# First attention of a two-layer encoder: filling products in pieces of three, weight slots exchanged singly

## Chip, core and metric

The kernel runs on one core of one Trainium2 chip. The metric is the device time of one execution in microseconds. A core has five engines that run side by side and meet only at semaphores: TensorE (PE in the profile; its weight loads are PEld), VectorE (DVE), ScalarE (ACT), GpSimd (POOL) and SyncE (SP), which issues most DMAs.

## What is computed

Two layers over a sequence of 1024 tokens of width 1024. The change lies in layer 0, whose mixer is:

```python
def even_mixer(xn, w_in, w_out, w_s, b_s, ln_g, ln_b, rel_bias):
    proj = xn @ w_in
    a_u, a_v, b_q, b_k, b_v, i_q, i_k, i_w = jnp.split(proj, splits, axis=-1)
    a_out = gmlp_spatial_gate(gelu(a_u), gelu(a_v), w_s, b_s, ln_g, ln_b)   # 1024 wide
    b_out = dsa_attention(q, k, v, iq, ik, iw, rel_bias)                    # 16 heads of 64
    return jnp.concatenate([a_out, b_out], axis=-1) @ w_out                 # 2048 -> 1024
```

`dsa_attention` picks 256 keys for each query with an indexer and attends over them with a relative bias. All 16 heads share one key and one value head. The output projection has 2048 inputs: the first 1024 (a_out) are there before the attention begins, the last 1024 are its result.

## The kernel before

Every product is done in split precision: each operand is a rounded high part and a low rest, and a product is three matmuls (high x high, high x low, low x high), or two where one operand is stacked. ScalarE rounds, VectorE or POOL subtract.

**The first attention** goes in 32 steps (i,b): head group i of four heads (i = 0 to 3), query block b of 128 tokens (b = 0 to 7), with b + 1 key tiles of 128. On TensorE (`pe_attn0`, L2637) a step is: the logits of the next step's heads 0 and 1, then for each key tile `st` four transposes of the probabilities (one per head, L2675) into one of two PSUM banks, a further head of the next step's logits behind tiles 1 and 2 (in short steps the rest behind the denominators), and from tile 2 on the value product of tile `st - 2` (two matmuls); then the denominators (L2684) and the last two value products. A transposed tile is copied and rounded by ScalarE (L1670), its low part is made by VectorE (L2237), and only that frees the bank and lets the value product go. VectorE also adds the mask to the logits and takes the row minimum, in a far part (L2202) and a near part of up to 256 keys (L2217), and takes ScalarE's exponentials (L1647) on from there by a reciprocal. It divides the output (L2271). ScalarE makes the output's high half (`out_high`, L1650) at key tile 2 of the next step, and POOL (`pool_attn0`, L1195) does the rest of the split in three operations (L1211 to L1216); POOL also makes each step's mask with bias (L1115). SP (`sp_attn`, L748) stores each split output to `cat_scratch`.

**The fills.** While this runs, TensorE also does half of the output projection: the 1024 rows of `w_out` that meet a_out. A fill k (0 to 31) is one token tile by one half of the columns, over four of the eight weight tiles: 4 x 3 = 12 matmuls into PSUM bank 7 (`fill`, L2617). Fills 0 to 15 use weight tiles 0 to 3, fills 16 to 31 tiles 4 to 7. The stationary side is a unit tile (token tile u = k // 2, two buffers, loaded by `fill_units` L740 two units ahead, once fill 2u - 3 has been taken). VectorE takes a finished fill out of PSUM (`take_fill`, L2222), adding for k >= 16 the part sum of fill k - 16, which SP has stored and loaded again (`after_fill`, L759). The places are set by `fill_steps` (L104): block 0 none, blocks 1 to 4 one fill, blocks 5 to 7 two, until 16 are done in a pair of head groups. So (1,6), (1,7), (3,6), (3,7) have none. Within a step, `fill_plan` (L2651) gives six matmuls ahead of the first transposes, and the rest behind in lumps of three or six:

```python
if len(fills) == 2:
    return {0: (fills[0], 0, 2), 1: (fills[0], 2, 4), 5: (fills[1], 0, 2), "end": (fills[1], 2, 4)}
k = fills[0]
return {0: (k, 0, 2), min(2, keys - 1): (k, 2, 3), "end": (k, 3, 4)}
```

**The weight slots.** Four slots hold split weight tiles. Tile n is rounded by ScalarE (`split_hi`, L402) once `tile_done(n - 4)` (L360) says that its slot is free, and subtracted by POOL (`split_lo`, L412). For the fills that is the end of fill 15 or 31. The exchange for fills 16 to 31 stands at the end of (1,6) and in (1,7) on both engines; that for the next weights at the end of (3,6) and in (3,7). The rest of the projection (`pe_out`, L2803) begins after step (3,7), with the last heads' outputs loaded as stationary operand `hidden`.

## Time and profile before

| what | value |
|---|---|
| median of 3 runs | 2545.99 us (2543.73 to 2550.15) |
| profiled execution: span from first to last instruction | 2557.9 us |
| PE busy | 2427.4 us, 95% of the span, 11680 matmuls |
| DVE, ACT, POOL busy | 1694.0, 1183.7, 1472.5 us (66%, 46%, 58%) |
| DMA | 369.64 MB, 145 GB/s |
| first attention | 466 to 808 us of the span |

For the profiled execution only the span is shown, no time around it; it is 11.9 us above the median of the runs. Busy time of PE counts matmuls that are pipelined, with modelled ends, so a high share does not say that nothing is lost between them; start times do. "Idle before" names what ended the idle time.

### The profile page before, as it was taken

To read this page: it belongs to the slowest core of one execution; us is meant where nothing else is said; L and a number is where in the kernel's file an instruction comes from. 1 tells how busy PE (TensorE), PEld (TensorE's weight loads), DVE (VectorE), ACT (ScalarE), POOL (GpSimd) and SP (SyncE) were. 2 spreads that over 40 slices of the span, in tenths; PEclk is the share of its full clock that TensorE was granted. 3 is DMA by queue.
4 is the path that set the end of the run, shared out by engine and by line. 5 is a ranking of instruction groups with operands and counts; after the bars stand their busy time and mean duration, and the time that the engine had idled before them with its cause. 6 is when DMAs were issued, how large, how long until landed. Compare 5 with 4: busy or idle time off the path is not lost.

```text
span 2557.9 us, 34068 instructions
## 1 busy us (share of the span) xinstructions
PE 2427.4 (95%) x11680; PEld 1996.4 (78%) x11680; DVE 1694.0 (66%) x2859; ACT 1183.7 (46%) x2025; POOL 1472.5 (58%) x817
## 2 busy tenths in 40 slices
PE   7899999898998999999999999989989999999997
PEld 5689888777776778888778887867777888878886
DVE  5469998667775486655666676167758655576676
ACT  5442533556664274444333236265555444434331
POOL 2111578645553129887678642357725887578951
PEclk9999999899999999999999999989999999999999
DMA  5380643733544624455644444755553454754343
GB/s 150 63 129 26 134 101 125 238 103 100 157 131 163 214 86 140 140 168 151 238 165 162 141 134 128 169 148 136 133 186 99 146 167 138 240 199 146 115 140 132
DMA packets 324244, 369.64 MB, mean 145 GB/s; under 512 B 13874, under 2 KB 222290, under 8 KB 322052
## 3 DMA queue, kind: packets, MB, share of 16 engines
q1 hardware_dynamic: 315476, 351.96, 47.2%
q10 hardware_dynamic: 8352, 15.21, 2.0%
q8 instruction: 83, 1.36, 0.2%
q0 software_dynamic: 272, 0.62, 0.1%
q14 instruction: 61, 0.50, 0.1%
HBM read 237.18 MB, written 130.55 MB: 144 GB/s over the span
## 4 chain that ended last, share of the span: by engine, by line
PE 75%; DVE 6%; POOL 6%; DMA 4%; issue 4%; ACT 4%; SPq 1%; POOLq 0%; DVEq 0%; ACTq 0%
PE ps L462 72%; PE ps L2675 2%; POOL attn_out_split L1239 1%; POOL attn_out L1237 1%; DMA hidden<-cat_scratch 1%; DMA cat_scratch<-attn_out_split 1%; ACT relu_scores L1508 1%; DVE masks L2068 1%; POOL w_split L417 1%; PE ps L579 1%; DMA h_operand_raw<-h_operand_scratch 1%; POOL attn_out_split L1235 1%; DVE logits L2202 1%; ACT junk L1349 1%; POOL attn_out_low L1232 1%
## 5 line engine op out<-in xcount | busy, mean ns | idle before, releaser
L462 PE MATMUL ps<-xn_T,w_split 128*128 128x512 f32 (+1 forms) x2928 | 679.7, 391 | 2.2 <-ACT x_sums L1386 1.4
L462 PEld LDWEIGHTS ps<-xn_T,w_split 128*128 128x128 f32 (+1 forms) x2928 | 548.6, 188 | 121.2 <-DVE xn_T L2001 2.7
L417 POOL TENSOR_TENSOR w_split<-w_raw,w_split 128x1024 fp32r<-128x1024 f32 x78 | 199.5, 2568 | 484.4 <-ACT w_split L410 484.0
L462 PE MATMUL ps<-w_operand,h_operand 128*128 128x512 f32 x2016 | 461.6, 391 | 11.4 <-DVE acc L2471 7.5
L462 PEld LDWEIGHTS ps<-w_operand,h_operand 128*128 128x128 f32 x2016 | 379.8, 189 | 93.2 <-issue 10.7
L1263 POOL TENSOR_TENSOR w_split<-w_raw,w_split 128x512 fp32r<-128x512 f32 x168 | 242.2, 1454 | 105.5 <-ACT w_split L1766 104.0
L462 PE MATMUL ps<-x_sums_high,w_split 128*128 128x512 f32 x896 | 285.0, 389 | 0.0
L1295 POOL TENSOR_TENSOR w_operand<-w_block,w_operand 128x2048 fp32r<-128x2048 f32 x42 | 207.4, 4938 | 110.9 <-ACT w_operand L1786 110.9
L2473 DVE TENSOR_TENSOR acc<-acc,ps 128x512 f32<-128x512 f32 x288 | 185.4, 680 | 123.7 <-PE ps L462 123.5
L462 PE MATMUL ps<-w_split,hidden 128*128 128x512 f32 x960 | 228.8, 400 | 18.2 <-DMA hidden<-cat_scratch 7.1
L462 PEld LDWEIGHTS ps<-w_split,hidden 128*128 128x128 f32 x960 | 184.8, 194 | 59.5 <-issue 10.6
L1773 ACT ACTIVATE h_operand<-h_operand_raw 128x2048 fp32r<-128x2048 f32 (+1 forms) x56 | 95.3, 1703 | 266.5 <-DMA h_operand_raw<-h_operand_scratch 266.5
L2403 DVE TENSOR_TENSOR h_operand<-h_operand_raw,h_operand 128x2048 fp32r<-128x2048 f32 (+1 forms) x56 | 165.8, 2962 | 58.8 <-ACT h_operand L1773 58.8
L462 PEld LDWEIGHTS ps<-x_sums_high,w_split 128*128 128x128 f32 x896 | 168.2, 188 | 35.0
L1766 ACT ACTIVATE w_split<-w_raw 128x512 fp32r<-128x512 f32 x168 | 104.9, 629 | 167.7 <-PE ps L462 163.9
L462 PE MATMUL ps<-x_sums_low,w_split 128*128 128x512 f32 x448 | 174.3, 389 | 0.0
L2088 DVE TENSOR_SCALAR_CACHE_REDUCE sel_flag<-masks,sel_bound 128x1024 uint8<-128x1024 f32 (+2 forms) x192 | 168.9, 942 | 1.1
L462 PE MATMUL ps<-w_split,unit_tile 128*128 128x512 f32 x576 | 159.3, 408 | 0.5
L1670 ACT ACTIVATE probs_T<-ps 128x512 fp32r<-128x512 f32 x144 | 83.3, 593 | 121.4 <-PE ps L2675 116.5
L1349 ACT ACTIVATE junk<-acc 128x1024 f32<-128x1024 f32 x60 | 63.5, 1059 | 154.9 <-DVE acc L2370 138.3
L2237 DVE TENSOR_TENSOR probs_T<-ps,probs_T 128x512 fp32r<-128x512 f32 x144 | 98.0, 687 | 48.6 <-ACT probs_T L1670 47.7
L1301 POOL TENSOR_TENSOR w_block<-w_block,w_block 128x2048 f32<-128x2048 f32 x24 | 129.2, 5385 | 0.0
(279 smaller groups left out, 4252.0 us busy)
## 6 DMA issues: line engine op xcount, KB each, us to landing
h_operand_raw<-h_operand_scratch SPq DMA_DIRECT2D x42, 1024.0 KB, 5.4
w_raw<-in_w SPq DMA_DIRECT2D x72, 512.0 KB, 8.0
w_block<-in_w SPq DMA_DIRECT2D x48, 512.0 KB, 5.7
q_scratch<-q_split SPq DMA_DIRECT2D x128, 128.0 KB, 2.6
cat_scratch<-attn_out_split SPq DMA_DIRECT2D x128, 128.0 KB, 2.6
w_raw<-in_w_in SPq DMA_DIRECT2D x30, 512.0 KB, 5.4
q_tile<-q_scratch ACTq DMA_DIRECT2D x58, 256.0 KB, 2.7
h_operand_scratch<-h_even SPq DMA_DIRECT2D x14, 1024.0 KB, 4.4
```

Source lines behind the costliest of these rows:

```text
L417: nc.gpsimd.tensor_tensor(whl[:, n0 % 4, 1, :], wraw[:, n0 % 4, :], whl[:, n0 % 4, 0, :].bitcast(F32), ALU.subtract).then_inc(w_lo, 1)
L462: return nc.tensor.matmul(out_ap, stat, mov, start=start, stop=stop)
L1263: nc.gpsimd.tensor_tensor(w1_split(L, k, 1), w1_operand(L, k), w1_split(L, k, 0).bitcast(F32), ALU.subtract).then_inc(w1_lo, 1)
L1295: nc.gpsimd.tensor_tensor(w_split2(z, 1), w_operand2(z), w_split2(z, 0).bitcast(F32), ALU.subtract).then_inc(w2_lo, 1)
L1301: nc.gpsimd.tensor_tensor(dst, x, y, op).then_inc(w2_sum, 1)
L1349: nc.scalar.activation(junk[:], src, ACT.Square, scale=0.5 * D ** -0.5, accum_out=ss[:, t:t + 1]).then_inc(n_jk, 1)
L1766: nc.scalar.activation(w1_split(L, k, 0), w1_operand(L, k), ACT.Copy).then_inc(w1_hi, 1)
L1773: nc.scalar.activation(h_split(z, 0), h_split(z, 1, raw=True), ACT.Copy).then_inc(h2_hi, 1)
L2088: return tick(nc.vector.tensor_scalar(flag[:, n % 2, 0:(picks[k] + 1) * P], row(picks[k]), bound[:, k:k + 1].bitcast(F32), None, op, ALU.a ...
L2237: nc.vector.tensor_tensor(pT[:, x % 4, 1, :], ps[:, 4 + y % 2, :], pT[:, x % 4, 0, :].bitcast(F32), ALU.subtract).then_inc(c_free, 1)
L2403: nc.vector.tensor_tensor(h_split(z, 1), h_split(z, 1, raw=True), h_split(z, 0).bitcast(F32), ALU.subtract).then_inc(h2_lo, 1)
L2473: last = nc.vector.tensor_tensor(e, e, o, ALU.add)
```

## The change

The 32 fills become 128 pieces of three matmuls (one weight tile each). A plan made once gives every piece its place: four ("start") between the first step's second and third logits; in block 0 two ahead of the transposes ("pre"), one behind the tile, one at the end; in block 1 one "pre", one behind each tile, one at the end; in blocks 2 to 7 one behind each of the last n key tiles, where n comes from a list, (more than b + 1 go to "pre", which happens only in (3,2)). Step (3,7) gets none. VectorE's `take_fill` moves with the last piece of each fill. A piece that is not the last of its fill raises `piece_done`, so a weight slot is free after its own last piece. ScalarE rounds the second set behind the last tiles of (1,7), the third behind the first tiles of (3,7). POOL does all four subtractions together in (1,7) and in (3,7), and at the start splits the fourth tile ahead of the mask of the third step.

```diff
+FIRST_PIECES = 4
+PIECES = [4, 4, 2, 3, 4, 4, 5, 6]
+PIECES_FIRST = [4, 4, 2, 2, 3, 3, 4, 6]
+PIECES_LAST = [4, 4, 4, 4, 5, 5, 6, 0]
+def piece_places(b, n):
+    if b == 0:
+        return ["pre", "pre", 0, "end"]
+    if b == 1:
+        return ["pre", 0, 1, "end"]
+    return ["pre"] * max(0, n - b - 1) + list(range(max(0, b + 1 - n), b + 1))
...
@@ tile_done
-            return fo_full, 16 * ((n - T_O0) // 4 + 1)
+            k, j = 16 * ((n - T_O0) // 4) + 15, (n - T_O0) % 4
+            return (piece_done, 3 * k + j + 1) if j < 3 else (fo_full, k + 1)
@@ pool_attn0
+        split_lo(pool, T_O0 + 3)
         pool.wait_ge(mask_ok, 8)
         mask_bias(2)
-        split_lo(pool, T_O0 + 3)
...
             if i % 2 and b == NB - 1:
-                n = T_O0 + 4 * (i // 2 + 1) + 2
-                split_lo(pool, n)
-                split_lo(pool, n + 1)
-                pool.wait_ge(w_lo, n + 2)
+                n = T_O0 + 4 * (i // 2 + 1)
+                for j in range(4):
+                    split_lo(pool, n + j)
+                pool.wait_ge(w_lo, n + 4)
...
-            if i % 2 and b == NB - 2:
-                n = T_O0 + 4 * (i // 2 + 1)
-                split_lo(pool, n)
-                split_lo(pool, n + 1)
-                pool.wait_ge(w_lo, n + 2)
@@ act_attn0
-                if i % 2 and b == NB - 1 and st in (4, 6):
-                    split_hi(act, T_O0 + 4 * (i // 2 + 1) + st // 2)
+                if i == 1 and b == NB - 1 and st > 4:
+                    split_hi(act, T_O0 + 4 + st - 5)
+                if i == 3 and b == NB - 1 and st < 4:
+                    split_hi(act, T_O0 + 8 + st)
...
+            if i == 1 and b == NB - 1:
+                split_hi(act, T_O0 + 7)
-            if i % 2 and b == NB - 2:
-                n = T_O0 + 4 * (i // 2 + 1)
-                split_hi(act, n)
-                split_hi(act, n + 1)
@@ dve_attn0
         for j in range(4):
             far(0, j)
             near(0, j)
+            if j == 1:
+                take_fills(PLAN0["start"])
...
-                if st == 2 and len(fills) == 2:
-                    take_fill(fills[0])
+                take_fills(PLAN0[g].get(st, []))
...
-            if fills:
-                take_fill(fills[-1])
+            take_fills(PLAN0[g].get("end", []))
@@ pe_attn0
+    def fill_piece(pe, p):
+        k, j = divmod(p, 4)
+        u, half, n = k // 2, k % 2, T_O0 + 4 * (k // 16) + j
+        pe.wait_ge(w_lo, n + 1)
+        if j == 0:
+            pe.wait_ge(fu_ld[u % 2], 32 * (u // 2 + 1))
+            pe.wait_ge(fo_free, k)
+            own_wait(pe)
...
+        mm(ps[:, 7, :], sh, wh, j == 0, False)
+        mm(ps[:, 7, :], sh, wl, False, False)
+        mm(ps[:, 7, :], sl, wh, False, j == 3).then_inc(fo_full if j == 3 else piece_done, 1)
...
-            if 0 in fills:
-                fill0(*fills[0])
+            pieces(g, "pre")
             pe.wait_ge(p_ok, 4 * g + 4)
             for st in range(keys):
-                if st and st in fills:
-                    fill0(*fills[st])
                 transposes(g, st)
                 if st and todo:
                     logits(g + 1, todo.pop(0))
+                pieces(g, st)
                 if st >= 2:
                     values(g, st - 2)
             denominators(g)
             for j in todo:
                 logits(g + 1, j)
-            if "end" in fills:
-                fill0(*fills["end"])
+            pieces(g, "end")
```

## Rows read from the trace of the kernel before

**Rows 1.** Busy time in stretches: PE, steps (1,0) to (1,7) and (2,2): stretch, length, busy.
```profile
555.53:558.69 3.16, 2.47 (x19) 1.00 0.67 200
558.69:565.61 6.92, 6.83 (x38) 1.00 0.43 103
565.61:573.38 7.77, 7.77 (x43) 1.00 0.40 101
573.38:583.22 9.84, 9.77 (x58) 1.00 0.55 141
583.22:594.37 11.15, 10.94 (x64) 1.00 0.30 72
594.37:610.37 16.00, 15.30 (x82) 1.00 0.45 115
610.37:624.57 14.20, 11.69 (x63) 1.00 0.42 127
624.57:636.35 11.78, 9.53 (x61) 1.00 0.19 47
...
646.65:657.28 10.63, 8.26 (x43) 1.00 0.40 83
```

**Rows 2.** The same, all engines (PE PEld DVE ACT POOL): (2,6), (2,7), (3,6).
```profile
694.28:712.05 17.77, 16.82 (x87) 12.96 (x86) 11.91 (x27) 9.48 (x17) 5.56 (x4) 1.00 0.49 141
712.05:726.92 14.87, 14.67 (x86) 11.59 (x84) 8.32 (x20) 7.09 (x18) 5.57 (x4) 1.00 0.50 140
781.77:795.95 14.18, 11.67 (x64) 8.40 (x63) 10.59 (x25) 9.38 (x18) 3.17 (x3) 1.00 0.20 46
```

**Rows 3.** Timeline of PE, start of (1,6): start, duration, work [idle before].
```profile
610.37 1.98 PE L462 MATMUL ps<-k_split,q_tile 128*128 128x512 f32 x8
612.19 1.04 PE L2675 MATMUL ps<-ident,logits 128*128 128x128 f32 x8
613.42 1.19 PE L462 MATMUL ps<-k_split,q_tile 128*128 128x512 f32 x4 [0.20 <-DVE row_min_all L2217]
615.65 0.66 PE L2675 MATMUL ps<-ident,logits 128*128 128x128 f32 x4 [1.03 <-DVE probs_T L2237]
```

**Rows 4.** Timeline of all engines, end of (2,6): value products, one key tile apart.
```profile
707.53 0.71 PE L462 MATMUL ps<-probs_T,v_split 128*128 128x512 f32 x2
...
708.43 0.71 PE L462 MATMUL ps<-probs_T,v_split 128*128 128x512 f32 x2
```

**Rows 5.** Timeline of DVE, start of (1,6): far part; low half of the probabilities.
```profile
611.72 0.96 DVE L2202 CUSTOM_DVE_ANT_0 logits<-ps,masks 128x768 f32<-128x768 f32 x1 [0.46 <-PE ps L462]
...
614.93 0.66 DVE L2237 TENSOR_TENSOR probs_T<-ps,probs_T 128x512 fp32r<-128x512 f32 x1
```

**Rows 6.** Groups of instructions by shape, 455 to 825 us: busy, mean ns.
```profile
L410 ACT ACTIVATE w_split<-w_raw 128x1024 fp32r<-128x1024 f32 x9 | 9.2, 1051 | 0.0
...
L2202 DVE CUSTOM_DVE_ANT_0 logits<-ps,masks 128x256 f32<-128x256 f32 x16 | 6.7, 419 | 2.0 <-POOL mask_bias L1115 1.9
```

**Rows 7.** Busy time in stretches, start of the attention; third from last: granted clock.
```profile
452.90:466.50 13.60, 9.55 (x38) 8.50 (x38) 5.58 (x20) 9.56 (x23) 13.37 (x6) 0.50 0.99 303
```

**Rows 8.** Timeline of PE, steps (0,1) and (0,2).
```profile
475.68 0.73 PE L462 MATMUL ps<-probs_T,v_split 128*128 128x512 f32 x2 [3.15 <-DVE probs_T L2237]
...
477.99 2.57 PE L462 MATMUL ps<-w_split,unit_tile 128*128 128x512 f32 x6
```

**Rows 9.** The chain of waits, start of the attention: start, length, what.
```profile
461.90 12.31 DMA cat_scratch<-a_out_split
```

**Rows 10.** Instructions of the tile unit_tile, 450 to 500 us.
```profile
L745 SPq DMA_DIRECT2D unit_tile<-cat_scratch x6: 443/758/1286, 456.6 to 491.7; - x6
...
DMA to landing us min/median/max: 5.9/6.8/8.2
```

**Rows 11.** Timeline of all engines, start of the attention: POOL's fourth weight slot.
```profile
464.26 2.39 POOL L417 TENSOR_TENSOR w_split<-w_raw,w_split 128x1024 fp32r<-128x1024 f32 x1
```

**Rows 12.** Timeline of POOL in (3,7): the output of (3,6) is split.
```profile
800.93 1.27 POOL L1214 TENSOR_TENSOR attn_out<-attn_out,attn_out_split 64x512 f32<-64x512 f32 x1 [3.35 <-ACT attn_out_split L1654]
```

**Rows 13.** Timeline of PE after the attention.
```profile
836.66 33.62 PE L462 MATMUL ps<-w_split,hidden 128*128 128x512 f32 x136 [6.02 <-DMA hidden<-cat_scratch]
```

More of the change, by code:

```diff
@@ L108, in fill_steps @@
         for b in range(NB):
[L109 to L114 removed]
+            n = 1 if 2 * NB - 2 < i * NB + b < 4 * NB - 1 else 0
             steps[i, b] = list(range(k, k + n))
@@ L117, in fill_steps, with piece_plan @@
     return steps
-FILL = [fill_steps(0), fill_steps(1)]
+FIRST_PIECES = 4
[8 more added lines that the diff above has]
+    return ["pre"] * max(0, n - b - 1) + list(range(max(0, b + 1 - n), b + 1))
+def piece_plan():
+    plan, done, p = {"start": list(range(FIRST_PIECES))}, {}, FIRST_PIECES
+    for g in range(HG * NB):
+        i, b = divmod(g, NB)
+        plan[g], done[i, b] = {}, [0] if g == 0 else []
+        for place in piece_places(b, (PIECES_FIRST, PIECES, PIECES, PIECES_LAST)[i][b]):
+            plan[g].setdefault(place, []).append(p)
+            if p % 4 == 3:
+                done[i, b].append(p // 4)
+            p += 1
+    assert p == 128
+    return plan, done
+PLAN0, DONE0 = piece_plan()
+FILL = [DONE0, fill_steps(1)]
 def mask_off(b):
@@ L335, in program @@
     fo_full, fo_free = S("fill_full"), S("fill_free")
+    piece_done = S("fill_piece_done")
     fo_sp = [S("fill_spill0"), S("fill_spill1")]
@@ L2238, in probs_low, with take_fills @@
                                     ALU.subtract).then_inc(c_free, 1)
+        def take_fills(pieces):
+            for p in pieces:
+                if p % 4 == 3:
+                    take_fill(p // 4)
         for j in range(4):
@@ L2242, in dve_attn0 @@
             near(0, j)
+            if j == 1:
+                take_fills(PLAN0["start"])
         for g in range(HG * NB):
             b, s = g % NB, g % 2
-            fills = FILL[0][divmod(g, NB)]
             todo = list(range(4)) if g + 1 < HG * NB else []
@@ L2635, in fill @@
             last.then_inc(fo_full, 1)
+    def fill_piece(pe, p):
[6 more added lines that the diff above has]
+            own_wait(pe)
+        sh = fu0[:, u % 2, j, 0, :]
+        sl = fu0[:, u % 2, j, 1, :]
+        wh = whl[:, n % 4, 0, half * 512:(half + 1) * 512]
+        wl = whl[:, n % 4, 1, half * 512:(half + 1) * 512]
+        mm(ps[:, 7, :], sh, wh, j == 0, False)
+        mm(ps[:, 7, :], sh, wl, False, False)
+        mm(ps[:, 7, :], sl, wh, False, j == 3).then_inc(fo_full if j == 3 else piece_done, 1)
     def pe_attn0(pe):
@@ L2646, in logits, with pieces @@
             qk(q_first[:, b, 1, j, :] if g < 4 else qst[:, b % 4, j, :], k2, KEYS0[b] * P, n % 2).then_inc(l_full, 1)
-        def fill0(k, j0, j1):
-            fill(pe, fu0, T_O0 + 4 * (k // 16), k, j0, j1)
-        def fill_plan(g):
-            fills = FILL[0][divmod(g, NB)]
-            keys = KEYS0[g % NB]
-            if len(fills) == 2:
-                return {0: (fills[0], 0, 2), 1: (fills[0], 2, 4), 5: (fills[1], 0, 2), "end": (fills[1], 2, 4)}
-            if not fills:
-                return {}
-            k = fills[0]
-            if keys == 1:
-                return {0: (k, 0, 2), "end": (k, 2, 4)}
-            return {0: (k, 0, 2), min(2, keys - 1): (k, 2, 3), "end": (k, 3, 4)}
+        def pieces(where, place=None):
+            for p in PLAN0[where] if place is None else PLAN0[where].get(place, []):
+                fill_piece(pe, p)
         def bank(y):
@@ L2694, in values @@
             mm(ps[:, 6, :], vv, pT[:, x % 4, 1, :], False, st == KEYS0[g % NB] - 1).then_inc(pv_done, 1)
-        for j in range(4):
-            logits(0, j)
+        logits(0, 0)
+        logits(0, 1)
+        pieces("start")
+        logits(0, 2)
+        logits(0, 3)
         pe.wait_ge(b_free, B_O0)
```

7 lines of the change are left out of this document (removed).

## The prediction

> **What bounds the kernel now.** I read the page first: one core, span 2557.9 us, TensorE busy for 95% of it (table above). The timed median is 2545.99 us, 11.9 us below the profiled span; nothing in the page explains that offset, so I work out a difference in the trace and take it off the median. About 0.3% (7.6 us) is what a measurement of this kernel can tell from no change.
>
> Then the busy time in stretches, cut at the steps of the first attention (466 to 808 us). Call a step (i,b): head group i, query block b, b+1 key tiles; it runs from the first product of the next step's logits to its own last value product. The reader is to see that the length follows the work on TensorE, plus holes. Work first. Eight logits products take 1.82 us, 0.229 each [rows 3]; four transposes and two value products, one key tile, take 0.90 us in a place without a wait [rows 4]; four transposes alone I count at 0.44. One fill is 12 products, 2.75 us; a piece is 0.69. Step (1,6) is then 7 x 0.90 + 0.44 (denominators) + 16 x 0.229 = 10.4 us of work and lasts 14.20: 3.8 us of holes. Step (1,7) is 8.1 of 11.78: 3.7. They hold no fill [rows 1]. Their twins (2,6) and (2,7) hold two fills each, 5.5 us of work, and are only 3.57 and 3.09 us longer [rows 2]: holes 1.9 and 1.3. The same arithmetic on steps (1,0) to (1,5) leaves 0.9, 0.6, 0.1, 0.75, 0.75 and 1.5 us. So the second head group has 12.0 us of holes; the fourth is like it. The third has 10.8: 1.9 and 1.3 in its last two steps, and 2.9 in (2,2), which lasts 10.63 with the work that (1,2) does in 7.77 [rows 1].
>
> The timeline of TensorE in (1,6) shows what the holes wait for: the third key tile's transposes start at 615.65, 5.28 us after the step's first product, of which 3.63 are work (8 logits products, 8 transposes, 4 products: 1.83 + 0.88 + 0.92) [rows 3]. VectorE sets that end: it starts the far part of the new logits at 611.72, takes 0.96 for it, does two heads of far and near, and only then the low half of the first probabilities, which frees the bank [rows 5]. The other 2.2 us lie later in the loop and before the denominators.
>
> **Part 1: pieces in the key loop.** The 384 filling products stay, so TensorE's work is the same and I count holes alone. Removed are the six products ahead of the first transposes in blocks 2 to 7 (except (3,2)); the gap before the third key tile is then as long as in (1,6), unless a piece stands behind an earlier tile. Scale the 5.28 us: with block 2's far part at 0.42 instead of 0.96 [rows 5, 6], twice, and 0.46 less of logits work ahead of it, it is 3.75 us; own work there is 0.92 + 0.88 + 0.46 and one piece, 2.95: hole 0.8 (0.95 with the first copy's wait). Between block 2 and 6 the same way: block 3 0.8, block 4 0.9, block 5 1.6, block 6 1.75; block 7, whose next logits are narrow, 1.05. Blocks 3 and 4 of the first head group have no piece behind tile 1: 1.5 and 1.6. The last head group has pieces behind tiles 0 and 1: 0.1, 0.1, 0.2, 0.9, 1.05 for blocks 2 to 6. Behind the third tile every tile of blocks 5 to 7 carries 0.69 us, and the later holes of (1,6), 2.2 us spread over five places, are covered; where a piece is absent (first group) a hole of up to 0.7 can stay. Blocks 0 and 1: 0.2 and 0.4, since block 0 gets four pieces where it had none.
> Sums, before to after: second head group 12.0 to 7.6, gain 4.4; fourth, without its last step, 8.3 to 3.0, gain 5.3; first, blocks 3 to 7, 6.2 to 7.5, loss 1.3.
>
> **Part 2: the exchange of the weight slots.** Before, the second set of four is rounded after fill 15, in (1,6) and (1,7), with no fill waiting. Now ScalarE rounds each slot (1.05 us) one key tile behind the piece that frees it, in (1,7), and POOL subtracts (2.39 us each [rows 6, 11]) back to back. With (1,7) at 13.3 us, the first slot is subtracted from 9.5 to 11.9 us into it, the fourth until 19.1. Pieces 64 and 65 find theirs; 66 waits 1.1 us and 67 0.8. Behind the four on POOL's queue stand the splitting of (1,7)'s output (3.3 us: two operations of 1.27 [rows 12] and a copy) and the mask of (2,3), as long as a slot; it is ready at 24.8, wanted at 26.7. So the 2.9 us hole of (2,2) goes, and the third head group goes from 10.8 to 9.4, gain 1.4. SP's stores of part sums, unit loads and first-part loads move with the fills; a unit is loaded two fills ahead, at least 10 us, against landings of 5.9 to 8.2 us [rows 10], so zero; where that lead shrinks to one fill the rest, some 2 us, would be TensorE's wait.
>
> **Part 3: four pieces at the start.** They stand between the second and third logits product of step (0,0), and wait for the first unit tile, two loads issued from 456.6 on, to landing 5.9 to 8.2 us [rows 10], that is about 464, and for POOL's fourth slot: it started at 464.26 behind a mask about as long as itself and now goes ahead of it, so it ends at about 464.3 [rows 11]. TensorE is idle there and at half clock (0.50 granted, 1.2 GHz) [rows 7], so 12 products take 2.8 to 5.1 us. The first transposes slip from 462 to some 472. But before, step (0,1) then sat 3.15 us until 475.68 behind a store of the gating stage that lands at 474.2, and the six products at 477.99 took 2.4 us where six take 1.4 [rows 8, 9]. Queuing all work after 464.3 one behind the other, I get the end of (0,2) at 489.2 with 14 pieces done, where it was 485.9 with 8: six pieces are 4.1 us, gain 0.9. Bounds: a full clock from 466.5 gives 2.5; half clock until 477 costs 3.
>
> **Part 4: the end.** TensorE's own end of (3,7) does not count. After the stage it waits 6.02 us at 836.66 for the last heads [rows 13], and that wait starts at POOL: the second last output is split from 800.93 (5.0 us into (3,7), which starts at 795.95 [rows 2, 12]), then four slots of 2.39 us, then the last output, its store and its load. Now ScalarE rounds three slots ahead of the high half that POOL waits for, where two stood: 6.05 us into the step. Loss 1.1, and what TensorE idles in (3,7) is free. Added waits: each piece looks at a semaphore of weights long since raised; bounds 0 and 1 us in all, I take 0.
>
> 96 pieces now raise a semaphore each. The eight logits products raise one each pair and run at 0.229 us [rows 3], so I see no price.
> The Trainium skill ("TensorE: Matmul & The Clock Gate", section "The cost: per-tile semaphore tail") has increments serialize at about 26 ns each: by it, an estimate of 2.5 us for 96, and a gain of 7.1 instead of 9.6. By that rule the products of rows 3 would be slower than others; they are not, and I stay with the row.
>
> **Sum:** 0.9 - 1.3 + 4.4 + 1.4 + 5.3 - 1.1 = 9.6 us. 2545.99 - 9.6 = 2536.4 us.
>
> **Rivals.**
> A. The late chain eats it: ScalarE rounding in the key loop of (3,7) and of (1,7) delays the copies that POOL and TensorE wait for by more than I count. For: POOL's chain decides the end, and each rounding is 1.05 us in the queue. Against: ScalarE is busy 9.5 of 17.8 us in a long step [rows 2]. Three more roundings' time is 3.2 us, plus 1 at the start: gain 5.4, 2540.6 us, within 0.3%. Chance 0.20.
> B. Every increment costs TensorE time, as a queue that serializes them would: 96 of them at a tenth of a product (0.026 us), 2.5 us: 2538.9, within 0.3%. Chance 0.05; rows 3 speak against it, and the skill's rule above is this one.
> C. Slower. The holes of the loop are no latencies but VectorE's and ScalarE's own rate, and pieces with their copies out of PSUM only stretch it; the cover ahead of the first transposes is gone. Then (0,6), (0,7), (2,6), (2,7) get the holes of (1,6) and (1,7), 4.3 us more in each head group, 8.7; block 5 goes from 1.5 to some 3.3, 7.2 over four groups; against these stand 2.9 from (2,2) and 2.1 from block 0. Net 11 us slower, 2557 us. It decides from 0.3 us more of hole per step on (9.6 over 32). For: VectorE is busy 11.9 and TensorE's own work 15.9 of 17.77 us in (2,6), so the reserve is only 4 us. Against: with two fills in the step the holes were smaller, not larger [rows 1, 2]. Chance 0.13.
> That the change doesn't do what it says can be left out: the same 384 products are in the list of pieces.
>
> **How the numbers follow.** Forecast 0.62, of which 0.07 falls under the 7.6 us; A 0.20, B 0.05, C 0.13. Faster 0.55, same 0.32, slower 0.13. Range: below, the start at +2.5 and block holes 30% smaller (6 us) give 2529; above, A together with the start at -3 gives 2544.5, and part of C to 2547. C's own time stays outside.
>
> **What would show it.** Step (1,6) at 10.4 + 3.45 + 1.7 = 15.6 us, (1,7) at 13.3, (0,7) at 13.4 and no half clock after about 470; in each of blocks 5 to 7 one long wait ahead of the third key tile and none over 0.3 us later; the second set's first pieces waiting 1 to 2 us for POOL in (2,0); POOL's last output split starting 18 us after (3,7). The forecast is wrong if (1,6) takes over 17 us, if the first step's transposes start after 475, or if TensorE's wait for the last heads grows by more than 2 us beyond what it gained before.

## The result and the profile after

The changed kernel is slower: 2560.13 us in the median of 4 runs (2556.20 to 2561.42), against 2545.25 us for the kernel before on the same chip. The ratio is 1.0048 with a 95% interval of 1.0035 to 1.0060, that is 9 to 15 us more. I had forecast 2536.4 us, 9.6 us less; the time lies outside the range of 2529 to 2547.

The traced execution of the changed kernel has a span of 2554.4 us and a time of 2556.2 us. The traced execution of the kernel before was a long one (span 2557.9 us); a second trace of it, taken with the experiments, has 2550.7 us. So the spans say little, and the comparison is made in the stage itself. From the first logits product to the first product of the output projection the kernel before takes 353.60 us, and 353.06 us in its second trace; the changed kernel takes 360.43 us, and 362.54 us in its second trace. That is 6.8 to 9.5 us of the 9 to 15. From step (0,3) on, the change takes 328.56 and 328.58 us, the kernel before 322.68 and 325.22. What stands ahead of (0,3) takes 31.87 and 33.96 us with the change, 30.92 and 27.83 before it. So the start of the stage moves by 2 to 3 us between traces of one kernel. What follows the stage moves too, by 5 to 6 us (1749.3 and 1744.7 us before, 1740.5 and 1734.5 with the change), and I can't assign what is left.

The busy times of the page after, first part (engine, busy us, share of the span, instructions), beside the table of before:

```profile
span 2554.4 us, 34066 instructions
...
PE 2417.3 (95%) x11680; PEld 1993.3 (78%) x11680; DVE 1700.2 (67%) x2859; ACT 1188.7 (47%) x2025; POOL 1483.2 (58%) x817
```

Nothing there tells what happened. The steps do. The busy time of TensorE in stretches, for steps (1,0), (1,2), (1,5) to (1,7), (2,0) and (2,2) of the changed kernel (stretch, length, busy, granted clock, DMA share, GB/s), answers to [rows 1]:

```profile
551.17:556.22 5.05, 5.05 (x32) 1.00 0.72 209
...
562.86:570.11 7.25, 6.85 (x37) 1.00 0.68 181
...
593.17:607.57 14.40, 12.60 (x69) 1.00 0.45 116
607.57:624.06 16.49, 14.64 (x78) 1.00 0.29 79
624.06:638.57 14.51, 13.10 (x79) 1.00 0.27 74
638.57:645.48 6.91, 5.59 (x31) 1.00 0.63 191
...
651.96:659.21 7.25, 6.87 (x37) 1.00 0.76 202
```

Step (1,6) takes 16.49 us where I had 15.6, (1,7) 14.51 where I had 13.3. Taking the work off each step as the prediction does (0.229 us a product, narrower ones in proportion, 0.109 a transpose, so these are counted numbers), the holes are:

| Holes on TensorE, us | before | forecast | after | of it, waits ahead of a fill |
|---|---|---|---|---|
| group 0, blocks 3 to 7 | 6.2 | 7.5 | 12.0 | 3.0 |
| group 1 | 12.0 | 7.6 | 13.1 | 4.3 |
| group 2 | 10.8 | 9.4 | 14.8 | 4.3, and 1.9 in (2,0) |
| group 3, blocks 0 to 6 | 8.3 | 3.0 | 6.7 | 3.1 |

The last column, 14.7 us without (2,0), is what the forecast does not have: 16 places, each counted from the last transpose's start to the fill's first product, less 0.109. The idle time that the profile itself shows there is a little less. The view of the waits of TensorE, 480 to 815 us of the changed kernel (what waits, what for, us in all, times, longest), names it:

```profile
PE ps L2707 <- DVE probs_T L2260: 15.5, 24, 1.2
PE ps L490 <- DVE part_sum L2254: 6.1, 8, 1.4
PE ps L490 <- DVE part_sum L2251: 6.0, 8, 1.0
PE ps L490 <- POOL w_split L445: 2.7, 3, 1.4
PE ps L490 <- DVE row_min_all L2240: 1.5, 8, 0.2
```

and the same view of the kernel before, 480 to 808 us:

```profile
PE ps L2675 <- DVE probs_T L2237: 13.3, 24, 2.0
PE ps L462 <- DVE row_min_all L2217: 2.5, 3, 2.1
PE ps L2684 <- issue: 2.3, 3, 0.9
PE ps L2684 <- DVE probs_T L2237: 1.1, 2, 0.6
```

The two `part_sum` rows are new: 12.1 us in 16 waits. A `part_sum` is VectorE's taking of a finished fill out of PSUM (L2251 for fills 0 to 15, L2254, with the first part added, for the rest). All fills are summed in one bank, number 7, so the first matmul of a fill waits until the fill before it has been taken (`fo_free`). The transposes wait 15.5 us in all, 2.2 more than before, though the prediction had the holes ahead of them shrink in groups 1 and 3.

One such wait in full. The timeline of TensorE in step (1,5) (start, duration, work [idle before, released by]):

```profile
598.10 0.66 PE L2707 MATMUL ps<-ident,logits 128*128 128x128 f32 x4 [1.01 <-DVE probs_T L2260]
...
602.53 0.94 PE L490 MATMUL ps<-w_split,unit_tile 128*128 128x512 f32 x3
603.31 0.63 PE L490 MATMUL ps<-probs_T,v_split 128*128 128x512 f32 x2
603.77 0.60 PE L2707 MATMUL ps<-ident,logits 128*128 128x128 f32 x4
604.99 0.93 PE L490 MATMUL ps<-w_split,unit_tile 128*128 128x512 f32 x3 [0.62 <-DVE part_sum L2251]
```

and that of VectorE at the same place:

```profile
603.44 0.69 DVE L2260 TENSOR_TENSOR probs_T<-ps,probs_T 128x512 fp32r<-128x512 f32 x1 [0.91 <-ACT probs_T L1693]
604.05 0.68 DVE L2251 COPY part_sum<-ps 128x512 f32<-128x512 f32 x1
605.04 0.69 DVE L2260 TENSOR_TENSOR probs_T<-ps,probs_T 128x512 fp32r<-128x512 f32 x1 [0.31 <-ACT probs_T L1693]
```

The last piece of a fill starts at 602.53 and is over by 603.5. VectorE first makes the low half of this tile's probabilities, copies the fill from 604.05 to 604.73, and the first piece of the next fill goes at 604.99: some 1.5 us after the bank was complete. In between TensorE has two value products and four transposes, 0.9 us. In the kernel before, two fills of a step stood several key tiles apart, and the taking was always over. With pieces behind every key tile, the fourth piece of one fill and the first of the next are neighbours.

### The profile page after: what moved, and what is told of

It is laid out like the page before. It is cut to its first block, busy times and chain, and to the rows that moved or that the text cites. A ratio compares the mean times of both kernels' runs of the same rounds, so it can differ in the third digit from the quotient of the medians.

```text
span 2554.4 us, 34066 instructions
## 1 busy us (share of the span) xinstructions
PE 2417.3 (95%) x11680; PEld 1993.3 (78%) x11680; DVE 1700.2 (67%) x2859; ACT 1188.7 (47%) x2025; POOL 1483.2 (58%) x817
## 4 chain that ended last, share of the span: by engine, by line
PE 60%; DVE 7%; POOL 5%; issue 4%; DMA 3%; ACT 3%; SPq 0%; DVEq 0%; POOLq 0%; ACTq 0%
PE ps L490 57%; POOL attn_out_split L1262 1%; POOL attn_out L1260 1%; PE ps L2707 1%; DVE logits L2225 1%; DMA cat_scratch<-attn_out_split 1%; DMA hidden<-cat_scratch 1%; DMA h_operand_raw<-h_operand_scratch 1%; POOL attn_out_split L1258 1%; POOL w_split L445 1%; POOL attn_out_low L1255 1%; DVE probs_T L2260 1%; DMA h_operand_scratch<-h_end_sums 1%; PE ps L2716 0%; DVE acc L1924 0%
## 5 line engine op out<-in xcount | busy, mean ns | idle before, releaser
L2430 DVE TENSOR_TENSOR h_operand<-h_operand_raw,h_operand 128x2048 fp32r<-128x2048 f32 (+1 forms) x56 | 171.5, 3063 | 60.3 <-ACT h_operand L1796 60.2
L490 PE MATMUL ps<-w_split,unit_tile 128*128 128x512 f32 x576 | 167.9, 411 | 19.8 <-issue 6.4
```

The lines of the kernel that those rows point to most:

```text
L490: return nc.tensor.matmul(out_ap, stat, mov, start=start, stop=stop)
L2430: nc.vector.tensor_tensor(h_split(z, 1), h_split(z, 1, raw=True), h_split(z, 0).bitcast(F32), ALU.subtract).then_inc(h2_lo, 1)
```

## The experiments

All ratios are against the kernel before, with a 95% interval; 0.1% is 2.5 us.

**Both kernels again.** The kernel before as it is, once, for a second trace; the changed kernel as it is, in 6 runs.

> The kernel before, unchanged, for a second trace. The first trace has a span of 2557.9 us while its timed median is 2545; the trace of the changed kernel has 2554.4 with a median of 2560. Theory: the first attention of this trace is as in the first (353 to 354 us from the first logits product at 455 to the first product of the output projection at 808.6), and the excess of the first trace sits in another stage that the change does not touch; the attention then explains only about 7 of the 15 us measured. Rival: the attention itself is shorter in a usual execution, by some 10 us (345 us), and the change costs 15 us all inside it.

> The changed kernel, unchanged, against the kernel before in more runs. By start times of the two traces its first attention is 6.8 us longer (360.4 against 353.6 us from the first logits product to the first product of the output projection), while the timed difference of four runs each was 15. Theory: the change costs what the stage shows, so the ratio comes out at 1.002 to 1.004 (5 to 10 us). Rival: something outside the stage costs another 8 us; then 1.005 to 1.006 stays.

Measured: the kernel before 2552.52 us, stage 353.06 us (353.60 in the first trace). The changed kernel 2557.74 us, ratio 1.0046 (1.0032 to 1.0060), stage 362.54 us. The loss repeats, a little above the 1.002 to 1.004 that I expected from the stage alone. The stage of the change differs by 2.1 us between its traces, all of it ahead of (0,3). That the two traces of the kernel before agree within 0.5 us is chance: the second is 3.1 us shorter ahead of (0,3) and 2.5 us longer behind it, of which 1.6 us are in step (2,2). The wait that ends at 475.68 in [rows 8] is 3.15 us in the first trace; in the second it is 0.78:

```profile
471.75 0.73 PE L462 MATMUL ps<-probs_T,v_split 128*128 128x512 f32 x2 [0.78 <-DVE probs_T L2237]
```

**The pieces kept, whole fills spaced apart.** The three matmuls of a piece still stand behind a key tile's transposes, but a step of block 2 or more holds exactly one fill, so that a fill's end and the next one's start are separated by a step's head. Step (0,2) has none and (2,7) two fills.

```
+    if (i, b) in ((0, 2), (HG - 1, NB - 1)):
+        return []
...
-    return ["pre"] * max(0, n - b - 1) + list(range(max(0, b + 1 - n), b + 1))
+    if b == 2:
+        return ["pre", 0, 1, 2]
+    if (i, b) == (2, 7):
+        return ["pre", 0, 1, 2, 4, 5, 6, 7]
+    return [b - 3, b - 2, b - 1, b]
```

> The changed kernel with another list of places: every step of blocks 2 to 7 holds the four pieces of exactly one fill, behind its last key tiles, so that a fill never begins within two key tiles of the end of the fill before (step (0,2) holds none, (2,7) two with a free tile between them). Theory, the handover of PSUM bank 7: the first piece of a fill waits until VectorE has taken the fill before, 12 us in 16 waits in the trace of the changed kernel and, by start times, 0.9 to 1.4 us at each of some 18 places. These waits go, and the stage gets 14 to 18 us shorter than in the changed kernel; against the kernel before it is 5 to 9 us faster. Rival, the head of the step: what costs is the missing cover ahead of the third key tile (about 1.7 us a step), which stays as it is here; then the time is within 3 us of the changed kernel's and the waits move to the transposes.

Measured, in 12 runs: 2545.92 us, ratio 0.9976 (0.9963 to 0.9990). Stage 346.78 us, 13.7 and 15.8 less than in the change's two traces. TensorE's waits, 480 to 800 us:

```profile
PE ps L2707 <- DVE probs_T L2260: 14.9, 20, 1.0
PE ps L490 <- POOL w_split L445: 2.1, 2, 1.1
PE ps L490 <- DVE row_min_all L2240: 1.5, 8, 0.2
```

The `part_sum` rows are gone and the transposes' waits are about what they were. This kernel has the same 128 pieces, the same increments and the same copies by VectorE. So neither small pieces nor VectorE's total work made the change slow; the order in which fills meet did.

**TensorE doesn't wait for the taking.** VectorE's copy (and the addition of the first part) reads an SBUF tile of the same size instead of the bank, and TensorE's wait for `fo_free` is left out. VectorE's instructions, their places and their shapes stay; their durations do not, as shown below. The first half of the output projection is left out of the result by this, so its time is read as that of the schedule alone.

```
-                nc.vector.tensor_copy(part[:, k % 2, :], ps[:, 7, :]).then_inc(fo_free, 1)
+                nc.vector.tensor_copy(part[:, k % 2, :], bias[:, 0:2, :].rearrange("p h n -> p (h n)")).then_inc(fo_free, 1)
... (the addition for k >= 16 likewise)
-            pe.wait_ge(fo_free, k)
```

> The changed kernel, where VectorE's copy of a fill out of PSUM reads a tile of the same size in SBUF instead, still after the fill is complete, and the next fill's first piece does not wait for it (what is left out: the first half of the output projection is not in the result). Same instructions on every engine, same places. Theory, handover: 12 to 18 us faster than the changed kernel, 0 to 3 us faster than the kernel before, the waits on part sums gone from TensorE's list. Rival: the waits were a shadow of VectorE's lateness and come back at the transposes; then under 4 us faster than the changed kernel.

Measured, in 12 runs: 2548.39 us, ratio 0.9995 (0.9980 to 1.0010). Stage 347.82 us, 12.6 less than the changed kernel's first trace and 14.7 less than its second. TensorE's waits, 480 to 800 us:

```profile
PE ps L2706 <- DVE probs_T L2260: 15.8, 25, 1.2
PE ps L490 <- DVE row_min_all L2240: 1.9, 9, 0.5
PE ps L490 <- POOL w_split L445: 1.6, 2, 1.1
PE ps L2715 <- DVE probs_T L2260: 1.0, 3, 0.5
```

The two missing rows were 12.1 us, the stage lost 12.6. Nothing of that size took their place. From (0,3) on, where the change's two traces agree, it is 316.33 us, 12.2 less. Meanwhile VectorE had more to do, not less: with a tile in SBUF to read, its takings are longer in the mean. Its groups for 455 to 810 us (busy us, mean ns; in the changed kernel both kinds take 0.68 us each, 21.9 us together):

```profile
L2254 DVE TENSOR_TENSOR part_sum<-bias,first_part 128x512 f32<-128x512 f32 x16 | 21.6, 1347 | 0.7 <-PE ps L490 0.7
L2251 DVE COPY part_sum<-bias 128x512 f32<-128x512 f32 x16 | 16.7, 1044 | 8.4 <-PE ps L490 8.4
```

So the stage gets 12.6 us shorter while VectorE's takings grow by 16.4 us: it was TensorE's wait that cost, and not VectorE's load. The timed gain against the change, 0.5%, agrees; against the kernel before, the stage is 5.5 us shorter and the time only 1.3 us (it may be 5.1 less or 2.5 more), so the time carries less of it than the trace shows.

**The taking doubled.** VectorE copies every fill twice into the same place, the second behind the first's end.

```
+                nc.vector.tensor_copy(part[:, k % 2, :], ps[:, 7, :]).then_inc(vl_f, 1)
+                dve.wait_ge(vl_f, GROUPS + k + 1)
                 nc.vector.tensor_copy(part[:, k % 2, :], ps[:, 7, :]).then_inc(fo_free, 1)
...
+            nc.vector.tensor_tensor(part[:, k % 2, :], ps[:, 7, :], first_part[:, k % 2, :], ALU.add).then_inc(vl_f, 1)
+            dve.wait_ge(vl_f, GROUPS + k + 1)
```

> The changed kernel, where VectorE takes every fill out of PSUM twice (0.69 us and a wait on itself of 0.2 us more each), which doubles the suspected cost. Theory, handover: the first piece of the next fill waits that much longer wherever it waited already (16 waits in the trace) and in a few places more, so 12 to 18 us slower than the changed kernel, all of it in waits of the filling products for the part sum. Rival, VectorE's time is covered and the copies only fill its idle time: under 4 us slower.

Measured, in 4 runs: 2576.85 us, ratio 1.0097 (1.0082 to 1.0113). Stage 380.05 us, 19.6 and 17.5 more than the two traces of the change, but by the ratios 12 to 13 us, inside the 12 to 18 expected. TensorE's waits, 480 to 815 us:

```profile
PE ps L490 <- DVE part_sum L2258: 13.2, 11, 2.2
PE ps L490 <- DVE part_sum L2253: 12.3, 9, 1.7
...
PE ps L490 <- DVE row_min_all L2240: 4.3, 12, 0.8
```

12.1 us have become 25.5 us, in 20 waits instead of 16: 0.7 us more on VectorE is 0.7 us more on TensorE wherever the wait was bare. The row of `row_min_all` has grown by 2.8 us, from 1.5: the near part of the logits now stands behind two copies. Together that is 16.2 us. From (0,3) on the kernel takes 344.44 us, 15.9 more than the change, so the rest of the difference lies ahead of (0,3), where the change's own traces differ by 2.1 us. With the wait taken out, spaced out and doubled, it is shown that this wait costs the stage some 12 us.

**The holes at a step's head.** The spaced kernel still had some 1.2 us of hole ahead of the third key tile's transposes in blocks 5 and 6. Here two of the four pieces stand ahead of that place in blocks 4 to 7, where one (block 4) or none did.

```
-    return [b - 3, b - 2, b - 1, b]
+    return {3: [0, 1, 2, 3], 4: [0, 1, 3, 4], 5: [0, 1, 3, 5], 6: [0, 1, 4, 6], 7: [0, 1, 4, 6]}[b]
```

> As e1_spaced, but in blocks 4 to 7 the first two pieces stand behind key tiles 0 and 1 and the other two late in the loop (tiles 4 and 6 in the long steps). If the handover and the hole ahead of the third key tile are both real and separate, the hole of 1.7 us in blocks 5 to 7 shrinks by the 1.38 us of two pieces, 12 steps and block 4 with about 0.9: another 12 to 18 us less than e1_spaced, so 18 to 25 us faster than the kernel before. If VectorE's rate is the bound (the rival), moving pieces forward only moves the waits: within 3 us of e1_spaced.

Measured, in 6 runs: 2535.23 us, ratio 0.9932 (0.9907 to 0.9956). Stage 335.50 us, 11.3 less than spaced, just short of the 12 to 18 expected. TensorE's waits, 480 to 788 us:

```profile
PE ps L2707 <- DVE probs_T L2260: 5.6, 11, 1.0
PE ps L490 <- POOL w_split L445: 2.5, 3, 1.3
PE ps L490 <- DVE probs_T L2260: 0.7, 4, 0.2
```

14.9 us in 20 waits become 5.6 in 11. Step (1,6) now takes 14.21 us with a whole fill in it, as long as it took with none before [rows 1]. This is what the change set out to do; it had its pieces behind the last n tiles of a step, and the wait is ahead of the third.

**The early start.** The eight pieces of step (0,0) all go to its end, and none stands between the logits.

```
-    plan, done, p = {"start": list(range(FIRST_PIECES))}, {}, FIRST_PIECES
+    plan, done, p = {"start": []}, {}, 0
...
-        for place in piece_places(b, (PIECES_FIRST, PIECES, PIECES, PIECES_LAST)[i][b]):
+        places = piece_places(b, (PIECES_FIRST, PIECES, PIECES, PIECES_LAST)[i][b])
+        for place in ["end"] * 8 if g == 0 else places:
```

> The changed kernel without the four pieces between the second and third logits product of the first step: the first eight pieces stand behind the denominators of step (0,0). What it tells is the price of the early place. Theory: TensorE is idle there anyway and the store of the gating stage that lands at 474 us bounds the next step, so the early place is worth nothing or little: the first transposes are back at 462 us, (0,3) starts within 1.5 us of where it does in the changed kernel, and the time is the same (within 3 us). Rival: the early place costs, since it holds up the first exponentials by 6 us: 3 to 5 us faster. Second rival: it gains 3 us.

Measured, in 6 runs: 2559.58 us, ratio 1.0042 (1.0027 to 1.0057), the change being at 1.0046. Stage 361.68 us, between the change's two. From the first logits product to the start of (0,3) it is 33.15 us, between the change's 31.87 and 33.96. So no run shows the early place to be worth anything. The kernel before takes 30.92 and 27.83 us there, with six pieces (4.1 us) less done. Whether having 14 pieces done by then gains or loses depends on the pair of traces: 3.1 us gained by the first, 2.0 lost by the second.

**The end, in the changed kernel.** POOL splits the last output after two of the last four slots instead of after all four.

```
-                for j in range(4):
+                m = 4 if i == 1 else 2
+                for j in range(m):
                     split_lo(pool, n + j)
-                pool.wait_ge(w_lo, n + 4)
+                pool.wait_ge(w_lo, n + m)
...
+            if (i, b) == (HG - 1, NB - 1):
+                split_lo(pool, T_O0 + 10)
+                split_lo(pool, T_O0 + 11)
+                pool.wait_ge(w_lo, T_O0 + 12)
```

> The changed kernel, where POOL splits the last step's output after two of the four next weight slots instead of after all four (the last two slots follow it). Theory, the late chain: TensorE's wait of 6.04 us for the last heads' outputs starts at POOL, so it shrinks by the two slots, 4.7 us, to 1 to 2 us, and the kernel is 4 to 5 us faster than the changed one. Rival: the load of the last heads, 14 us from issue to landing, is bound by its queue, and the wait stays: no difference.

Measured, in 12 runs: 2553.32 us, ratio 1.0024 (1.0016 to 1.0033). TensorE after the stage, first in the changed kernel (first trace), then in this one:

```profile
813.86 22.03 PE L490 MATMUL ps<-w_split,hidden 128*128 128x512 f32 x96 [1.40 <-POOL w_split L445]
841.93 38.41 PE L490 MATMUL ps<-w_split,hidden 128*128 128x512 f32 x159 [6.04 <-DMA hidden<-cat_scratch]
```

```profile
839.67 10.52 PE L490 MATMUL ps<-w_split,hidden 128*128 128x512 f32 x45 [1.93 <-DMA hidden<-cat_scratch]
```

The wait for the last heads falls from 6.04 (4.70 in the second trace of the change) to 1.93 us.

**The end, in the kernel before.** The same two edits alone in the kernel before, with its own order of the roundings kept.

```
-            if i % 2 and b == NB - 1:
+            if i == 1 and b == NB - 1:
                 n = T_O0 + 4 * (i // 2 + 1) + 2
...
+            if (i, b) == (HG - 1, NB - 1):
+                split_lo(pool, T_O0 + 10)
+                split_lo(pool, T_O0 + 11)
+                pool.wait_ge(w_lo, T_O0 + 12)
```

> The kernel before, where POOL splits the last step's output ahead of the last two weight slots (the edit of e6_end_chain alone). If the late chain is what it was in the changed kernel, TensorE's wait for the last heads (6.0 us) shrinks by 4 to 5 us and the kernel is 3 to 5 us faster than before (ratio 0.998 to 0.9988). Rival: the gain came from the changed kernel's own timing there, and here it is under 1 us.

Measured, in 11 runs: 2545.89 us against 2551.04 for the kernel before beside it, ratio 0.9978 (0.9969 to 0.9988). Stage 353.04 us, as before. The line that answers to [rows 13]:

```profile
830.82 19.56 PE L462 MATMUL ps<-w_split,hidden 128*128 128x512 f32 x85 [0.54 <-DMA hidden<-cat_scratch]
```

6.02 us of wait (4.82 in the second trace) are now 0.54, and the time is 3.1 to 7.9 us less. That agrees with the wait, but not all of it need be the wait. During it TensorE's granted clock falls to 0.50, and the products from 836.66 to 850 us run at a mean of 0.80. In this kernel those from 830.80 to 850 us run at 1.00 throughout.

**All of it together.** The early places, the end, and ScalarE's roundings moved: in (1,7) behind tiles 1, 3, 5, 7, in (3,7) behind tiles 3 to 6.

```
...
-                if i == 1 and b == NB - 1 and st > 4:
-                    split_hi(act, T_O0 + 4 + st - 5)
-                if i == 3 and b == NB - 1 and st < 4:
-                    split_hi(act, T_O0 + 8 + st)
+                if i == 1 and b == NB - 1 and st % 2:
+                    split_hi(act, T_O0 + 4 + st // 2)
+                if i == 3 and b == NB - 1 and 3 <= st < 7:
+                    split_hi(act, T_O0 + 8 + st - 3)
...
-            if i == 1 and b == NB - 1:
-                split_hi(act, T_O0 + 7)
```

> e2_early with the end of e6_end_chain, and with ScalarE's roundings spread: in (1,7) behind key tiles 1, 3, 5 and 7 (each behind its piece, so POOL starts some 4 us earlier), in (3,7) behind tiles 3 to 6, after the high half that POOL waits for. Theory: TensorE's wait for POOL in (2,0), 3.8 us in e2_early, goes to under 1, the end chain gives 4 to 5: 6 to 9 us faster than e2_early and 20 to 24 us faster than the kernel before (ratio 0.991). If only the end chain works, 4 us faster than e2_early.

Measured, in 5 runs: 2524.33 us, ratio 0.9903 (0.9888 to 0.9919). Stage 336.08 us, no less than without the moved roundings (335.50). Step (2,0) still has 4.65 us of holes. POOL shows why; its timeline from the end of (1,6) on, then two pieces of TensorE's:

```profile
618.68 1.28 POOL L1243 TENSOR_TENSOR attn_out<-attn_out,attn_out_split 64x512 f32<-64x512 f32 x1 [4.01 <-ACT attn_out_split L1682]
...
621.52 2.39 POOL L1143 TENSOR_TENSOR mask_bias<-bias,masks 128x1024 f32<-128x1024 f32 x1 [0.20 <-POOL attn_out_split L1245]
623.99 9.34 POOL L445 TENSOR_TENSOR w_split<-w_raw,w_split 128x1024 fp32r<-128x1024 f32 x4
```

```profile
628.75 0.96 PE L490 MATMUL ps<-w_split,unit_tile 128*128 128x512 f32 x3 [1.30 <-POOL w_split L445]
...
631.07 1.57 PE L490 MATMUL ps<-w_split,unit_tile 128*128 128x512 f32 x3 [0.92 <-POOL w_split L445]
```

Rounding earlier is no use, against what I expected (under 1 us in (2,0)): POOL waits 4.01 us for the output of (1,6), splits it, makes a mask, and only then comes to the four slots. The two waits are 2.2 of the 4.65 us (idle time in the profile). Behind them TensorE's granted clock is down: it is 0.53 in the mean from 631.0 to 634.1 us, where 11 products and transposes keep TensorE busy for 3.03 us. The three products at 631.07 take 1.37 us instead of 0.69. At the full clock the same work would take about half of that, so some 1.5 us of the holes, an estimate, are the clock and not the waits.

**The exchange in POOL's queue.** Two of the four subtractions stand ahead of that 4 us wait. To free the slots in time, (1,7) gets no fill, and (0,2) gets one.

```
...
+            if (i, b) == (1, NB - 2):
+                split_lo(pool, T_O0 + 4)
+                split_lo(pool, T_O0 + 5)
+                pool.wait_ge(w_lo, T_O0 + 6)
             pool.wait_ge(oh_ok, g + 1)
...
-                if i == 1 and b == NB - 1 and st % 2:
-                    split_hi(act, T_O0 + 4 + st // 2)
+                if i == 1 and b == NB - 1 and st in (0, 1, 3, 5):
+                    split_hi(act, T_O0 + 4 + (st + 1) // 2)
```

> e7_all, where step (1,7) holds no fill (the fill goes to (0,2), which had none), so that the weight slots are free a step earlier; ScalarE rounds the second set behind tiles 0, 1, 3 and 5 of (1,7), and POOL subtracts the first two in its idle time of 4 us before the high half of (1,6)'s output. Theory, POOL's queue sets the wait of step (2,0): in e7_all its four subtractions start at 624 us, behind an output split and a mask, whatever ScalarE does, and (2,0) has 4.7 us of holes; here 2 of 4 are done earlier, the holes of (2,0) go to under 1 and (1,7) gets some 1 to 2 us of its own: 2 to 4 us faster than e7_all. Rival: the roundings early in (1,7) cost in the key loop what the exchange gives back: within 1.5 us of e7_all.

Measured, in 4 runs: 2524.55 us, ratio 0.9898 (0.9883 to 0.9913). Stage 331.96 us, 4.1 less than the one before; 1.5 us of that lie in step (0,0), which the edit doesn't touch. In the timeline of POOL the subtractions stand where they were meant to:

```profile
616.65 4.72 POOL L445 TENSOR_TENSOR w_split<-w_raw,w_split 128x1024 fp32r<-128x1024 f32 x2 [1.11 <-ACT w_split L438]
...
626.75 4.73 POOL L445 TENSOR_TENSOR w_split<-w_raw,w_split 128x1024 fp32r<-128x1024 f32 x2
```

The holes of (2,0) fall from 4.65 to 1.24 us, and its granted clock is 1.00 throughout. Those of (1,7), now without a fill, rise from 2.00 to 4.55, and 1.7 us go from (0,2). By the times the two kernels can't be told apart, where I had expected 2 to 4 us. Both beat the kernel before by about 1%, and the changed one by 1.4%.

## Why the prediction was wrong

The step that failed is the opening of part 1: "The 384 filling products stay, so TensorE's work is the same and I count holes alone", and then holes at two places only, ahead of the third tile's transposes and later in the loop. A third place, ahead of a fill's first product, was not in the count. Its wait stood in the code (`pe.wait_ge(fo_free, k)` in `fill_piece`, as in the old fill), the copy's 0.7 us stood in the trace, and one bank for all fills could be read from both. I took a wait that cost nothing before as one that costs nothing at any distance, and never asked how much work must stand between a fill's end and the next one's start. The runs show 12.1 us of idle time there, in 16 waits.

Step (1,6) shows it in small: 10.4 + 3.45 + 1.7 = 15.6 us forecast, 16.49 measured, and 0.8 of the 0.9 between them is that wait, counted as in the table (0.62 idle in the profile). By the parts of the sum, from the first trace of each kernel:

- **First group, blocks 3 to 7:** forecast 1.3 us lost, measured 5.8; 3.0 of the holes are waits for the taking. Blocks 5 and 6 have some 1.2 us ahead of the third tile and 0.35 at the logits before it, where I had scaled 1.6 and 1.75 together from (1,6). In block 7 it is 1.0, where I had 1.05.
- **Second group:** forecast 4.4 gained, measured 1.1 lost. Without the 4.3 us of new waits it would be 3.2 gained. The holes without them are 8.8 us, and in the kernel whose TensorE doesn't wait they are 9.0; the forecast had 7.6. So a second term, the holes that stay, was too low as well: by 0.6 to 1.5 us in each of the four groups. In (1,3) to (1,7), what they hold beyond the known waits is in gaps of under 0.15 us each, spread over the step.
- **Third group:** forecast 1.4 gained, measured 4.0 lost, with 4.3 us of new waits. The waits for the exchanged slots in (2,0) came to 1.9 us, as forecast (1.1 + 0.8), and the hole of (2,2) fell from 2.9 to 0.9 us: with six products fewer the step takes 7.25 us.
- **Fourth group:** forecast 5.3 gained, measured 1.6, with 3.1 us of new waits.
- **Start:** forecast 0.9 gained, measured 3.1 to the start of (0,3); by the second traces of both it is 2.0 lost. The 12 early products took 4.45 us at 460.91, inside my 2.8 to 5.1, and the first transposes came at 468.38, not at 472: the queue that I had put behind 464.3 was too long. But the term rested on one execution: the 3.15 us before 475.68, which the sum took for given, are 0.78 us in the second trace of the kernel before, and the half clock behind them (0.50 from 476.8 to 480.2) is not there at all (1.00 from 464.5 to 480.8).
- **End:** forecast 1.1 lost. POOL begins the second last output's split 5.7 us into (3,7), forecast 6.05, and the wait for the last heads is 6.04 us, as before. From (3,7)'s start to the product behind that wait it is 41.43 us, 40.71 before: 0.7 lost. The mechanism was right.

These close: 3.1 - 5.8 - 1.1 - 4.0 + 1.6, and 0.7 more of length in (3,7) itself, is 6.9 us of loss, the stage's 6.8. The start of the attention on TensorE, the line of before being the waits in [rows 8]:

```profile
460.91 4.45 PE L490 MATMUL ps<-w_split,unit_tile 128*128 128x512 f32 x12 [6.42 <-issue]
...
468.38 0.60 PE L2707 MATMUL ps<-ident,logits 128*128 128x128 f32 x4
```

And the exchange and the end on POOL, which answer to [rows 11, 12]:

```profile
634.73 9.43 POOL L445 TENSOR_TENSOR w_split<-w_raw,w_split 128x1024 fp32r<-128x1024 f32 x4 [0.69 <-ACT w_split L438]
...
806.20 1.27 POOL L1242 TENSOR_TENSOR attn_out<-attn_out,attn_out_split 64x512 f32<-64x512 f32 x1 [4.06 <-ACT attn_out_split L1677]
```

**"What would show it"** had the right lines for the wrong reason. It named one long wait ahead of the third tile and none over 0.3 us later; the later one, 0.6 to 1.4 us ahead of a fill's first product, is what the forecast was missing. It also said that the forecast is wrong if (1,6) takes over 17 us. (1,6) takes 16.49, below that bound, and the forecast is wrong all the same: I had set the bound for one step without asking what the same excess in 16 places comes to.

**The rivals.** C, slower, had the right sign with another mechanism: it held VectorE's and ScalarE's rate to be the limit. The spaced kernel has the same copies and products and a stage 13.7 us shorter, and without TensorE's wait it is 12.6 us shorter with 16.4 us more work for VectorE, so the rate is not the limit. C did name the copies out of PSUM, but as load, not as something to wait for, and its price of 11 us near the measured one is a coincidence. A, the late chain, is refuted by the wait for the last heads: 6.04 and 4.70 us, before 6.02 and 4.82. B, a price for each increment, finds nothing: step (3,2) has no hole to speak of in either kernel and holds one fill in both. Busy time of TensorE in it, before, and then after, where the fill is four pieces with an increment each:

```profile
737.01:744.78 7.77, 7.77 (x43) 1.00 0.54 137
```

```profile
739.18:746.94 7.76, 7.76 (x43) 1.00 0.75 203
```

7.77 and 7.76 us, with three increments more. The Trainium skill ("TensorE: Matmul & The Clock Gate", section "The cost: per-tile semaphore tail") gives about 26 ns for each increment, for the tail behind a pack of small matmuls. Carried over to this place, an estimate, three increments would add 0.08 us. This case's trace does not show it for increments inside a running stream of products.

The chance of 0.13 for slower was too small. The prediction asked which waits the change removes, and which waits the copies stand in front of, but not whether the new order brings a producer and the next user of one buffer close together.

## What to carry to other kernels

Before splitting filling work into finer pieces, list the buffers through which it leaves its engine, and for each the time from the last write to the next permitted write: here 1.5 us with one bank, of which the copy is 0.7. Then look at how much other work of the same engine lies between the end of one fill and the start of the next; here 0.9 us, so each such boundary costs 0.6 us, and up to 1.4 where VectorE comes to the copy late (in (3,6) it finishes the next step's logits first and starts at 792.16, 1.4 us after the fill's end). Whole fills with a gap between them, and their pieces ahead of the step's longest wait, took the same idea from 0.5% slower to 0.7% faster. On an engine that works in order, what the next stage waits for goes ahead of what is only prepared.

## What I had not expected

- **The order of the pieces outweighs their size.** Three placements of the same 128 pieces have stages of 360.4, 346.8 and 335.5 us, a spread of 25 us, with the same products.
- **A second bank was not tried.** The stage uses all eight: logits in 0 to 3, transposes in 4 and 5, values in 6, fills in 7. The wait itself is a need: the Trainium skill ("PSUM — Partial Sum Buffer", section "PSUM bank collisions raise a hardware error") says that two engines at the same time at the same partitions of one bank are an error, and that data are spoiled by it; no run here shows that.
- **At the exchange of the slots, POOL's order counts for more than ScalarE's.** Rounding the slots earlier changed nothing (336.08 against 335.50 us); moving two subtractions of 2.4 us ahead of a wait took 3.4 us out of (2,0), part of it because the granted clock no longer fell there. Freeing the slots for it put 2.6 us into (1,7).
- **The end of the stage was worth 0.2% by itself**, in the kernel before as in the changed one, by moving two subtractions behind an output: the wait of 6.02 us at [rows 13] fell to 0.54, and the half clock behind it went with it.
- **Still open:** the trace gives 6.8 to 9.5 us of the loss, the ratio 9 to 15. With TensorE's wait taken out, the stage is 5.5 us shorter than before, yet the ratio is 0.9995; with the exchange mended, the stage is 4.1 us shorter and the time the same. What follows the stage takes from 1731 to 1749 us in the traces of all these kernels, and 5 to 6 us more or less in two traces of one and the same. What moves it stays open.
